# Reordering VectorE's and ScalarE's queues in the prompt recurrence of a two-layer hybrid decoder kernel

## The reference, cut to what matters

```python
xs = c + (shifted - c) * shift_mu
r, k, v, xw, xa = split(xs)
w = -softplus(-(decay_w0 + tanh(xw) @ decay_lora_b)) - 0.5
decay = exp(-exp(w))
a = sigmoid(iclr_a0 + xa @ iclr_lora_b)
kk = k * key_k;  kk = kk / max(norm(kk), 1e-12)
k = k * (1 + (a - 1) * key_a)
S = S * decay + (S @ -kk) (kk*a)^T + v k^T        # one step per token
y = S r;  y = groupnorm(y) + sum(r*k*bonus) * v;  y = y * silu(gate)
```

## Time and profile before

| | |
|---|---|
| median of the runs | 4656.27 us |
| profiled execution, its own time | 4654.4 us |
| its span | 4652.5 us |
| TensorE busy | 4041.4 us, 87% |
| VectorE busy | 2060.1 us, 44% |
| ScalarE busy | 1734.2 us, 37% |
| GpSimd busy | 519.0 us, 11% |
| mean DMA rate | 88 GB/s |

### The profile page before, as it was taken

The page is one execution under the profiler, slowest core; times in us unless marked ns, Lnnn a source line. Parts: engine busy times, 40 slices in busy tenths (PEclk is TensorE's granted clock), DMA queues, the critical chain, the costliest instruction groups (busy, mean ns, idle before and its releaser), DMA issues.

```text
span 4652.5 us, 113506 instructions
## 1 busy us (share of the span) xinstructions
PE 4041.4 (87%) x49138; PEld 3517.5 (76%) x49138; DVE 2060.1 (44%) x4539; ACT 1734.2 (37%) x3547; POOL 519.0 (11%) x273
## 2 busy tenths in 40 slices
PE   7999998778887888888989999977888878888798
PEld 7999997677774655567989999976777745655588
DVE  6111111666654565555231111126666555555465
ACT  2000001666654665662110000016666556666421
POOL 5222220000000000002032222200000000000111
PEclk9999998799998999998999999988999989998899
DMA  3111111111112543434321111111111134543442
GB/s 138 69 69 69 70 77 61 34 46 38 38 45 86 162 139 119 138 116 152 118 86 71 74 69 69 65 68 35 42 38 41 46 110 144 171 142 88 150 142 93
DMA packets 224389, 410.46 MB, mean 88 GB/s; under 512 B 32402, under 2 KB 132756, under 8 KB 210068
## 3 DMA queue, kind: packets, MB, share of 16 engines
q1 hardware_dynamic: 208916, 313.75, 21.4%
q10 hardware_dynamic: 14976, 89.46, 4.8%
HBM read 296.39 MB, written 106.76 MB: 87 GB/s over the span
## 4 chain that ended last, share of the span: by engine, by line
PE 67%; DVE 12%; ACT 9%; issue 5%; PEld 3%; DMA 2%; SPq 2%; POOL 0%; ACTq 0%; DVEq 0%; PEldq 0%
PE psum L2146 10%; PE psum L2143 10%; PE psum L2145 10%; PE psum L1372 4%; PE psum L1400 4%; PE psum L715 3%; PE psum L1388 2%; PE psum L1136 2%; ACT arena L1176 2%; PE psum L712 2%; PE psum L1706 2%; PE psum L1707 2%; PE psum L1708 2%; PE psum L786 1%; DVE arena L520 1%
## 5 line engine op out<-in xcount | busy, mean ns | idle before, releaser
L2143 PE MATMUL psum<-x_hi,w_parts 128*128 128x416 f32 x2640 | 929.5, 352 | 42.4 <-POOL w_parts L2064 18.0
L2146 PE MATMUL psum<-x_hi,w_parts 128*128 128x416 f32 x2640 | 934.0, 354 | 0.0
L2145 PE MATMUL psum<-x_lo,w_parts 128*128 128x416 f32 x2624 | 917.6, 350 | 0.0
L2076 DVE TENSOR_TENSOR arena<-psum,arena 128x416 f32<-128x416 f32 x330 | 195.1, 593 | 1238.5 <-PE psum L2146 1234.7
L334 ACT ACTIVATE arena<-arena 128x256 f32<-128x256 f32 x16 | 8.2, 514 | 1477.3 <-DVE arena L458 1477.3
L2143 PEld LDWEIGHTS psum<-x_hi,w_parts 128*128 128x128 f32 x2640 | 497.4, 188 | 49.4 <-POOL w_parts L2064 20.5
L2145 PEld LDWEIGHTS psum<-x_lo,w_parts 128*128 128x128 f32 x2624 | 494.3, 188 | 8.9 <-issue 0.6
L2146 PEld LDWEIGHTS psum<-x_hi,w_parts 128*128 128x128 f32 x2640 | 496.9, 188 | 3.1
L1279 DVE TENSOR_SCALAR_CACHE_REDUCE arena<-psum 128x512 f32<-128x512 f32 (+3 forms) x640 | 357.6, 608 | 285.8 <-PE psum L1372 153.5
L1400 PE MATMUL psum<-arena 128*128 128x128 f32 x2176 | 309.5, 284 | 64.0 <-ACT arena L1185 46.7
L1372 PE MATMUL psum<-arena 64*128 64x512 f32 (+3 forms) x1280 | 325.8, 613 | 40.1 <-DVE arena L1279 22.2
(11 more groups left out here) (348 smaller groups left out, 6716.9 us busy)
## 6 DMA issues: line engine op xcount, KB each, us to landing
out_proj_t<-arena ACTq DMA_DIRECT2D x66, 1040.5 KB, 4.1
arena<-in_cache_k SPq DMA_DIRECT2D x256, 256.0 KB, 2.8
arena<-in_cache_v SPq DMA_DIRECT2D x256, 256.0 KB, 3.0
arena<-in_w_in SPq DMA_DIRECT2D x66, 512.0 KB, 3.5
arena<-out_proj_t SPq DMA_DIRECT2D x96, 257.0 KB, 3.3
arena<-out_proj_t SPq DMA_DIRECT2D x24, 1024.0 KB, 5.6
x_res<-in_x SPq DMA_DIRECT2D x10, 1664.0 KB, 12.7
m_raw<-mixed_t SPq DMA_DIRECT2D x8, 1664.0 KB, 10.7
```

The lines of the kernel that those rows point to most:

```text
L2076: dve.tensor_tensor(ost[:, b % 2, 1 + g * TG:1 + (g + 1) * TG], bank[q % banks_of(l)][:, 0:TG], RSTD[:, cols(g)], ALU.mult).then_inc(p_ev, 1)
L2143: pe.matmul(bank[q % n][:, 0:TG], w_hi[:, b % 3, k, :], x_hi[:, g, k, :], start=(k == 0), stop=False)
L2145: pe.matmul(bank[q % n][:, 0:TG], w_hi[:, b % 3, k, :], xl, start=False, stop=False)
L2146: mm = pe.matmul(bank[q % n][:, 0:TG], w_lo[:, b % 3, k, :], x_hi[:, g, k, :], start=False, stop=(k == KT - 1))
```

## The change

On VectorE, `mix_out(r)` now stands ahead of the first score mask, and `masked(u, 1)` right behind that mask, ahead of the token shift. The keys (`sV_KF`, `sV_RKB`) move from between the two state updates' first and L628 to behind the second state update, and the reciprocal norms (`sV_MX`, `sV_RC`) move up to them, ahead of `F_REC`, `F_YN`, `sV_R` and `sV_K`; the positions are renumbered to match. On ScalarE the low-rank copy moves from the slot's end to right behind `mixes(m)`, and the low-rank tanh to the very end of the slot, behind the copies for the next inversion. TensorE's and SyncE's programs are as before, but for the number that TensorE waits for with `sV_RC`. No instruction is added or taken out.

```diff
@@ -245,7 +245,7 @@
         in_raw, in_lora, in_gate, stored = mark("in_raw", 3, 16), mark("in_lora", 1, 16), mark("in_gate", 1, 16), mark("stored", 1, 16)
 
         sA_CK, sA_CR, sA_CV, sA_TW, sA_TA, sA_KS, sA_E, sA_EI, sA_MM, sA_SQ = range(1, 11)
-        sV_XK, sV_XR, sV_XV, sV_LD, sV_SCAN, sV_KF, sV_RKB, sV_R, sV_K, sV_MX, sV_RC, sV_KKN, sV_A, sV_BB, sV_B, sV_BV = range(1, 17)
+        sV_XK, sV_XR, sV_XV, sV_LD, sV_SCAN, sV_KF, sV_RKB, sV_MX, sV_RC, sV_R, sV_K, sV_KKN, sV_A, sV_BB, sV_B, sV_BV = range(1, 17)
         sT_ZW, sT_ZA, sT_SS, sT_RN, sT_BO = range(1, 6)
         pA, pV, pT = mark("prep_scalar", 10), mark("prep_vector", 16), mark("prep_tensor", 5)
         lA, lV = mark("lora_scalar", 2), mark("lora_vector", 1)
@@ -327,11 +327,13 @@
                         i_ = act.activation(cop[:, j, c, :], raw[:, j, c, 1:TQ + 1], ACT.Copy, scale=dpr[:, m % 2 * 2 + c, j:j + 1])
                     pA.inc(i_)
 
-            def lora(lt):
+            def lora_copy(lt):
                 in_lora.wait(act, lt, 1)
                 if lt:
                     lV.wait(act, lt - 1, 1)
                 lA.inc(act.activation(copl[:, :], rawl[:, 1:TQ + 1], ACT.Copy, scale=dpr[:, 0, 3:4]))
+
+            def lora_tanh(lt):
                 lV.wait(act, lt, 1)
                 lA.inc(act.activation(lin[0:64, :], lin[0:64, :], ACT.Tanh))
                 lA.close()
@@ -373,6 +375,8 @@
                 u, t, n, q, r, m, lt = roles(s)
                 if m is not None:
                     mixes(m)
+                if lt is not None:
+                    lora_copy(lt)
                 if t is not None:
                     wT.wait(act, t, 1)
                     for h in range(2):
@@ -433,8 +437,6 @@
                         i_ = act.activation(ysb[:, c, :], b4(4)[:, c, :], ACT.Identity, bias=prm[:, c, 10:11], scale=prm[:, c, 9:10])
                     fA.inc(i_)
                     fA.close()
-                if lt is not None:
-                    lora(lt)
                 if u is not None:
                     x_out(u, 4)
                     for k in (xA, xtA):
@@ -445,6 +447,8 @@
                     mvA.inc(act.activation(hc(AMV[:, n % 2, :, CH:P]), pair(0, 0), ACT.Copy))
                     for k in (mvA, x0A):
                         k.close()
+                if lt is not None:
+                    lora_tanh(lt)
 
         def rwkv_gpsimd(pool, l):
             pool.memset(E[:, :, :, 0:1], 1.0).then_inc(r_once, 1)
@@ -588,15 +592,15 @@
                 if q is not None:
                     post(q, F_MEAN)
                     post(q, F_YC)
+                if r is not None:
+                    mix_out(r)
                 if n is not None:
                     scores(n, scB, BS[:, n % 3, :, 1:3, :], smB)
-                if r is not None:
-                    mix_out(r)
+                if u is not None:
+                    masked(u, 1)
                 if m is not None:
                     mixed(m, sV_XK)
                     mixed(m, sV_XR)
-                if u is not None:
-                    masked(u, 1)
                 if n is not None:
                     scores(n, scK, SK[:, n % 3], smK)
                 if m is not None:
@@ -619,9 +623,6 @@
                     x0D.close()
                 if t is not None:
                     z_new(t, 0)
-                if m is not None:
-                    prep(m, sV_KF)
-                    prep(m, sV_RKB)
                 if t is not None:
                     gA.wait(dve, t, 2)
                     w = slice(t % 2 * P, t % 2 * P + P)
@@ -632,14 +633,15 @@
                 if t is not None:
                     z_new(t, 1)
                     zV.close()
+                if m is not None:
+                    for k in (sV_KF, sV_RKB, sV_MX, sV_RC):
+                        prep(m, k)
                 if q is not None:
                     post(q, F_REC)
                     post(q, F_YN)
                 if m is not None:
                     prep(m, sV_R)
                     prep(m, sV_K)
-                    prep(m, sV_MX)
-                    prep(m, sV_RC)
                 if lt is not None:
                     lora(lt)
                 if u is not None:
```

## The result

The changed kernel takes 4486.96 us (median of four executions) against 4656.25 us, a ratio of 0.9638 with a 95% interval of 0.9625 to 0.9651. The forecast was 4495 us. Its profiled execution has a span of 4489.1 us, 163.4 us less than before. One execution of the kernel of experiment 9 took 5243.77 us at a granted clock of 0.715, where the others have 0.94 to 0.95, and is left out of that kernel's median.

A forecast was written before the change was run, and what follows sets the result against it. It took TensorE's own work plus its waits to bound a recurrence slot. Slots 2 to 12 gave 134 us and other slots 27 us, 161 us in all: 4493 us profiled, 4495 us median, range 4460 to 4550.

The forecast's parts named there:

- Bound: Recurrence slots 2 to 12: TensorE's own work plus waits, mostly for VectorE's mask; about 2.4 us of slot 10 are clock.
- Old outputs and level-1 mask: VectorE at the slot's head: moving both forward ends TensorE's level-1 wait, gain 1.50 us.
- the cover: VectorE's 1.82 us idle before the score mask hides 1.33 us of old outputs; otherwise up to 1.33 us delay.
- Keys and norms: VectorE behind the second state: level 3 gains its whole 2.87 us; about 0.74 us of wait stays before L686.
- the rival "norms": ScalarE does not come forward by 1.5 us, TensorE waits 1.4 us more a slot: 4526 us; chance 0.11.
- Low-rank copy: ScalarE's slot head: copy hidden there, level-4 wait falls from 2.05 to 0.2 us, gain 1.85 us in slots with lt.
- Tanh: ScalarE's slot end: table load and tanh delay the next head, 0.15 us in an odd slot, without a drain.
- The sum: Slots at 30.4 us give 134 us over both layers, other slots 27 us: 161 us in all, 4495 us.
- Feed: TensorE's gaps without a releaser grow to 2.3 us a slot, as in slot 14: 4528 us; chance 0.13.
- Larger gain: No gap grows, full clock also in slots 0 and 1; 29.6 us a slot, 40 us outside: 4464 us; chance 0.08.
- No change: Another chain, the attention's first loads, ends the stage: 4656 us; chance 0.02.
- Slower, by the clock: Remaining waits hold TensorE's clock low for longer; at 40% of the work 4770 us; chance 0.03.

The follow-up runs named there:

- experiment 9: Changed kernel with roots and norms ahead of the keys, sV_K behind the level-4 mask, sum of squares behind the level-2 mask, tanh before x_out(u, 4): 4471.47 us.
- experiment 2: Kernel before with only the keys and reciprocal norms moved behind the second state update: 4549.97 us, ratio 0.9759.
- experiment 4: Kernel before with the keys moved behind the second state update but the norms left behind sV_K: 4624.82 us, ratio 0.9925.
- experiment 5: Changed kernel with mix_out behind masked(u, 1) instead of ahead of the first score mask: 4510.73 us against 4487.76 us beside it.
- experiment 1: Kernel before with only mix_out ahead of the first score mask and masked(u, 1) right behind that mask: 4625.64 us, ratio 0.9914.
- experiment 7: Changed kernel with roots and norms ahead of the keys, sV_K behind the level-4 mask, sum of squares F_VAR behind the level-2 mask: 4470.65 us, ratio 0.9602.

## Why the prediction was right, by its own steps

**Bound.** Right. Of the 144 us in slots 2 to 12, 111 us were time in which TensorE stood and 33 us clock. The 2.4 us of clock put down for slot 10 are 30.77 - 28.11 = 2.7 us. The prediction saw the low clock behind the level-3 wait, and most of the clock came back when this wait and the norms' went together (experiment 2), none of it when the one only moved into the other (experiment 4). Why some waits came with a low clock and others, as experiment 5's, did not, is open.

**Old outputs and level-1 mask.** Right in the mechanism: in slot 10 level 1 gained its 1.50 us, and the cover was as told, since without it the old outputs come back as a wait (experiment 5). The size was too large by the new wait at level 2. "Gain 1.50 us" is 1.1 to 1.3 us a slot in the part alone (experiment 1).

**Keys and norms.** Right in the mechanism and in what is late next. Forecast was a rest of 0.74 us before the norms' product, measured is 0.60 us. Experiment 4 shows the step on which it hung. The condition of the rival "norms", that ScalarE does not come forward, did not hold. L362 ended 20.6 us after slot 10's start (1234.05 - 1213.43), and the same instruction, now L364, ends 19.3 us after it (1167.51 - 1148.18):

```profile
1166.43 1.08 ACT L364 ACTIVATE arena<-arena 128x256 f32<-128x256 f32 x2
```

That is 1.3 us earlier where 1.5 us were forecast. TensorE's own level-2 start moved by 1.3 us too, 0.38 us of wait included.

**Low-rank copy.** Right: the part alone gave 33 us, and 30 us were expected. Forecast was a rest of 0.2 us before level 4, and it is 0.26 us. L717 starts 0.77 us behind L778 in slot 10 and 0.51 us behind it in slot 9, which has no low rank:

```profile
1142.65 0.69 PE L778 MATMUL psum<-arena 64*64 64x64 f32 x32
1143.16 1.11 PE L717 MATMUL psum<-arena 64*64 64x64 f32 x32
...
1171.93 0.69 PE L778 MATMUL psum<-arena 64*64 64x64 f32 x32
```

**Tanh.** Right, 0.15 us expected at an odd head, 0.2 us found. There is no drain behind the table load in its new place either:

```profile
1118.98 1.28 ACT L338 ACT_TABLE_LOAD   x1
1120.27 0.42 ACT L338 ACTIVATE arena<-arena 64x256 f32<-64x256 f32 x1
```

**The sum.** The total came out closer than its parts: 161 us were forecast, the profiled execution gave 163.4 us and the medians 169.3 us. Two terms were off in size, 10 us too little inside slots 2 to 12 and 8 us too much outside, and that they cancel is luck. The gaps without a releaser were taken at 0.8 us a slot, with 0.5 us as the lower bound; they came to 1.9 + 0.5 + 0.4 = 2.8 us in the first layer's eleven slots, 0.25 us each, less than the 5.3 us of before. In the second execution of the changed kernel that was profiled they were 6.6 us, 0.6 us a slot. So the bound's lower end was near, and slot 14 was the wrong guide: the gaps did not grow as the waits went. The norms' wait was also put too high for a mean slot, as 0.74 us in each is 8.1 us, and 5.4 us were measured. A slot was forecast at 30.4 us and is 29.9 us (328.38 / 11) and 30.0 us: 144 us in place of 134. Slots outside 2 to 12 were put at 27 us and gave 19.1 us in slots -2 to 1 (163.4 - 144.3) and 1.5 us in slots 13 to 15. Slot 0 gave 4.1 and 3.4 us in the two layers instead of 6 us, slot 1 gave 3.6 and 2.6 us (forecast 3), and slots -2 and -1 gave 3.9 and 1.4 us (forecast 3.6 with slot -3). Why the second layer's slots gave less was not looked into.

**Not foreseen.** Level 2 got a wait of up to 0.38 us in some slots. In experiment 1 it takes back up to a quarter of the level-1 gain. In slot 10 VectorE goes from the level-1 mask through the second score masks, the token shift, the scan and the sum of squares to the level-2 mask without a pause. What is left of that wait in the changed kernel is about 1.3 us in eleven slots, too little to show in the times (experiment 7).

**Rivals.** "Feed" did not happen: the gaps were 0.2 to 0.6 us a slot, not 2.3. "Larger gain" was right that no gap grows and that slots 0 and 1 run at full clock (1.00 in both), and a slot came near its 29.6 us, but its 4464 us needed 40 us outside the eleven slots, where some 20 us came. "No change" and "Slower, by the clock" are refuted by the time and by the clock, which went up.

## What to carry to other kernels

Where several engines run one hand-written order, read each wait of the bound engine together with what stands just ahead of the awaited instruction on its own engine; a short instruction that others wait for belongs right behind its own input, and work with ready inputs belongs into the idle time ahead of it. Then ask what the bound engine waits for next, and move that too in the same step: here the keys alone gave 34 us and the keys with the norms 109 us. Ask also what the moved work pushes back on its own engine, as with the new wait at level 2. Price the clock from two stretches of equal work at different granted clocks, and do it for each wait by itself: here the clock gave back 22 us beside 58 us of waits in one place and 3 us beside 23.5 us in another. Compare versions in the stretch that was changed, since the rest of the program moved by 10 us and more from one execution to the next.

## What the runs showed of the hardware that was not expected

Gaps of TensorE without a releaser did not grow when the waits between matmuls went: 5.3 us in the first layer's eleven slots before, 2.8, 6.6 and 2.0 us in three profiled executions of the changed kernel, though the same 10120 matmuls came in 328 us instead of 403 us. With the second layer's slots it was 11.5 us before and 7.1, 9.2 and 6.4 us after. What these gaps are is open.

Not every wait cost clock. With the keys moved and the norms left behind (experiment 4) TensorE stood for 125 us in both layers' slots 2 to 12, and its busy time was within 0.5 us of the kernel before; with the norms moved too it stood for 85 us and was busy 22 us less. In experiment 5 it stood 23 us longer than in the changed kernel beside it, and was busy 4 us less.

And with 14.7 us of the 328 us idle instead of 72 us of 403 us, the granted clock held at 0.99 to 1.00 through both recurrences.
